# Moving the constants, residuals and tokens of a two-block network to other SBUF addresses

## The reference

```python
mod = silu(c) @ w_mod + b_mod                      # six vectors of 1024: shifts, scales, gates
h, hc = modulate(x, ...), modulate(ctx, ...)       # rmsnorm(t) * (1 + scale) + shift
qkv, z, ba, sc_p, fn_u = split(h @ w_in)           # the same for hc
o_lat = bidir_gated_delta(...)                     # chunked gated delta rule, both directions
merged = g0 * y_dn + g1 * y_sc + g2 * y_fn         # delta, short-convolution and Fourier branches
x = x + gate1 * (merged @ w_o)
x = x + gate2 * swiglu(modulate(x, ...))           # width 2816
x = rmsnorm(x, final_g)
```

## Time and profile before

| | |
|---|---|
| three runs | 2008.36, 2011.93, 2009.1 us; median 2009.1 |
| profiled execution | 2004.89 us, span 2003.1 us |
| instructions | 34324, of these 14672 matmuls |
| TensorE busy | 1833.5 us, 92% of the span |
| VectorE, ScalarE, GpSimd busy | 968.2, 773.9, 463.2 us |
| mean granted TensorE clock | 0.959 |
| moved by DMA | 261.76 MB, 131 GB/s in the mean |

### The profile page before, as it was taken

One profiled execution on the slowest core, in us unless ns is written; L12 is line 12 of the kernel. 1 busy time (PEld: TensorE's weight loads), 2 busy tenths in 40 slices (PEclk: granted clock), 3 DMA queues, 4 the chain that ended last, 5 costly groups with the idle time before them and its releaser, 6 DMA issues.

```text
span 2003.1 us, 34324 instructions
## 1 busy us (share of the span) xinstructions
PE 1833.5 (92%) x14672; PEld 1557.8 (78%) x14672; DVE 968.2 (48%) x1666; ACT 773.9 (39%) x1332; POOL 463.2 (23%) x226
## 2 busy tenths in 40 slices
PE   5998998888899999999798879999999989689999
PEld 3777897877689997877686457787888776479998
DVE  1648425565543335345767754222231247954343
ACT  3453523333345555223532234222222343655443
POOL 0235212122034432211310011121222211013443
PEclk7999998999889998999899989999999999999999
DMA  8343343222465544221210114323322337025553
GB/s 320 156 162 136 105 154 131 86 107 86 170 238 195 190 169 166 101 94 67 85 64 1 64 64 147 126 97 119 122 105 100 111 137 271 3 71 203 190 189 127
DMA packets 36581, 261.76 MB, mean 131 GB/s; under 512 B 4048, under 2 KB 4176, under 8 KB 6224
## 3 DMA queue, kind: packets, MB, share of 16 engines
q1 hardware_dynamic: 36432, 259.58, 35.9%
HBM read 258.51 MB, written 1.05 MB: 130 GB/s over the span
## 4 chain that ended last, share of the span: by engine, by line
PE 77%; DVE 13%; ACT 4%; issue 3%; DMA 1%; POOL 1%; SPq 0%; DVEq 0%; ACTq 0%
PE ps L808 18%; PE ps L810 18%; PE ps L809 18%; PE ps L835 2%; PE ps L859 2%; PE ps L1308 1%; PE ps L1311 1%; DVE msq L2365 1%; PE ps L1077 1%; PE ps L825 1%; PE ps L1065 1%; PE ps L826 1%; PE ps L827 1%; PE ps L922 1%; PE ps L867 1%
## 5 line engine op out<-in xcount | busy, mean ns | idle before, releaser
L726 POOL TENSOR_TENSOR wl<-raw,wh 128x1024 fp32r<-128x1024 f32 (+1 forms) x179 | 428.2, 2395 | 1335.1 <-ACT wh L1417 1335.1
L808 PE MATMUL ps<-h_hi,wh 128*128 128x256 f32 (+1 forms) x1696 | 554.6, 327 | 5.2 <-POOL wl L726 3.8
L810 PE MATMUL ps<-h_hi,wl 128*128 128x256 f32 (+1 forms) x1696 | 544.8, 321 | 0.0
L809 PE MATMUL ps<-h_lo,wh 128*128 128x256 f32 (+1 forms) x1696 | 543.9, 321 | 0.0
L1417 ACT ACTIVATE wh<-raw 128x1024 fp32r<-128x1024 f32 (+1 forms) x330 | 342.4, 1041 | 392.3 <-PE ps L810 283.8
L808 PEld LDWEIGHTS ps<-h_hi,wh 128*128 128x128 f32 x1696 | 322.8, 190 | 35.2 <-POOL wl L726 8.4
L809 PEld LDWEIGHTS ps<-h_lo,wh 128*128 128x128 f32 x1696 | 322.5, 190 | 27.4 <-issue 2.7
L810 PEld LDWEIGHTS ps<-h_hi,wl 128*128 128x128 f32 x1696 | 321.9, 190 | 26.2
L1910 DVE TENSOR_TENSOR wl<-raw,wh 128x1024 fp32r<-128x1024 f32 (+1 forms) x151 | 187.9, 1244 | 240.2 <-ACT wh L1417 225.1
L808 PE MATMUL ps<-gh,wh 128*128 128x256 f32 (+1 forms) x528 | 168.2, 319 | 0.0
L810 PE MATMUL ps<-gh,wl 128*128 128x256 f32 (+1 forms) x528 | 166.9, 316 | 0.0
(11 more groups left out here) (404 smaller groups left out, 2808.8 us busy)
## 6 DMA issues: line engine op xcount, KB each, us to landing
raw<-in_mod SPq DMA_DIRECT2D x72, 1024.0 KB, 5.0
raw<-in_ffn_in SPq DMA_DIRECT2D x66, 1024.0 KB, 4.8
raw<-in_ffn_out SPq DMA_DIRECT2D x24, 1024.0 KB, 4.8
raw<-in_w_in SPq DMA_DIRECT2D x16, 1024.0 KB, 4.9
raw<-in_w_gate SPq DMA_DIRECT2D x12, 1024.0 KB, 4.9
raw<-in_w_ab SPq DMA_DIRECT2D x12, 1024.0 KB, 4.8
raw<-in_ffn_out SPq DMA_DIRECT2D x12, 768.0 KB, 4.4
raw<-in_w_at SPq DMA_DIRECT2D x5, 1024.0 KB, 4.9
```

The costliest lines, as they stand in the source:

```text
L726: nc.gpsimd.tensor_tensor(wl[e % SPLIT][:, 0:entries[e]["words"]], part(e), wh[e % SPLIT][:, 0:entries[e]["words"]].bitcast(F32), ALU.subt ...
L808: nc.tensor.matmul(b[:, cols], wh[e % SPLIT][:, w], xh(k), start=(k == 0), stop=False)
L809: nc.tensor.matmul(b[:, cols], wh[e % SPLIT][:, w], xl(k), start=False, stop=False)
L810: ins = nc.tensor.matmul(b[:, cols], wl[e % SPLIT][:, w], xh(k), start=False, stop=(k == nk - 1))
```

## The change

Two lines are added in the allocation. Each raises the count of words to the next multiple. No instruction is added, removed or moved, and no other offset is changed; tiles placed by `at` follow `phase_at`, `h_at`, `arena` and `spare`.

```diff
     small = sb("small", [P, NSMALL + (-NSMALL) % 8])
+    words[0] += -words[0] % 64
     call = sb("const_all", [P, NCALL])
     phase_at = words[0]
     c1 = sb("const_1", [P, NC1])
...
     words[0] += T - L - P - 8
+    words[0] += -words[0] % 256
     res_c = sb("res_c", [P, KD, L])
     res_l = sb("res_l", [P, KD, L])
     h_at = words[0]
```

## The result

The changed kernel takes 2022.55 us in the median of 7 runs (2017.45 to 2028.94), the kernel before 2011.16 in 7 runs beside it: the ratio is 1.0059, with a 95% interval of 1.0042 to 1.0076. It is slower, by some 12 us; the forecast was no change that can be told.

What follows compares the result with a forecast made beforehand. The prediction took TensorE's rate through 14672 matmuls to bound the kernel (busy 92%), plus stretches where VectorE finishes last. Its terms summed 0 + 0 + 0 + 0, so it forecast the unchanged median, 2009.1 us, range 2003.5 to 2015.

Steps and rivals of the forecast that it cites:

- the one under TensorE: 7536 matmuls streaming moved tiles: same step at either address, 117.8 against 117.7 ns; taken as 0, bound 1.1 us either way.
- The sign of being wrong that the prediction named: Dense stretches' matmul count in 10 us moved by one or more everywhere, or a moved-tile operation with another median.
- is not fixed by the address: TensorE's surplus over plain column time: 91 or 87 matmuls in 10 us with the same tokens at the same addresses.
- Rival 1: Tokens and weights at the same position modulo 256 words slow 7536 matmuls by 2 ns each, 15.1 us, giving 2024; 5%.
- Rival 2: Operands starting mid 128-byte piece cost one piece more; matmuls lose the surplus, 42 + 53 us, giving 1914; 2%.
- The other terms: Everything beside TensorE: VectorE and ScalarE 0 (bound 0.5 us), GpSimd 0 (bound 2.1), DMA 0 (bound 2).
- VectorE, ScalarE and GpSimd 0: Operations on moved tiles keep their times: 0, bounds 0.5 us for VectorE and ScalarE, 2.1 us for GpSimd's 40 level products.
- the constants 0: Constants move from word 12688 to 12736; their loads fall under the transfers taken as 0, with no separate time priced.
- the reading of the edit as one shift by 48 words: Everything from the constants up moves 48 words (192 bytes); the second new line adds nothing.
- DMA: Loads and stores of moved tiles, 7.5 of 260 MB: 0, bounds 0.1 us by pieces of a row, 2 us by whole transfer.

Runs made afterwards that it cites:

- all_up_48: Every tile, weight buffers too, moved up 48 words against the kernel before, so the token-to-weight distance stays 208; ratio 1.0003 (0.9977 to 1.0029).
- weights_208_rest_256: Against the kernel before, weight buffers and `small` moved up 208 words, all else 256, making the distance 0; ratio 1.0075 (1.0052 to 1.0097).
- before_again: The kernel before, unedited, run again as a control; ratio to the kernel before 1.0006 (0.9985 to 1.0027).
- const_only_48: Against the kernel before, constants and small tiles behind them up 48 words; residuals, tokens and arena up 256, keeping distance 208; ratio 0.9986 (0.9967 to 1.0005).
- after_again: The changed kernel, unedited, run again as a control; ratio to the kernel before 1.0068 (1.0042 to 1.0093).
- res_only_48: Against the kernel before, only residuals, tokens and arena moved up 48 words, constants left in place, distance 0; ratio 1.0069 (1.0051 to 1.0088).
- by_stretch: Against the kernel before, distances chosen by stretch: middle layer 0, first block, attention layer and outer feed-forwards 16 (modulo 64 words); ratio 1.0005 (0.9988 to 1.0022).
- h_hi_0_h_lo_16: Against the kernel before, `h_hi` and the arena set at distance 0 modulo 64 words to the weights, `h_lo` alone at 16; ratio 1.0076 (1.0039 to 1.0112).
- dist_240: Against the kernel before, residuals, tokens and arena up 32 words, distance 240 (48 modulo 64); ratio 1.0049 (1.0027 to 1.0071).

## Why the prediction was wrong

**The step that failed** is the one under TensorE: "no difference", 0 with a bound of 1.1 us either way. It compared the by-token stretch, where `wh` and `wl` stream and the tokens are loaded, with the feed-forward, where `gh` and `gl` stream and `wh` and `wl` are loaded. I took that as today's position against tomorrow's. It is so for one operand, but what counts is the distance of the two. That was -208 words in the one and 208 in the other, 48 and 16 modulo 64, and 0, which the change brings, was in neither. `all_up_48` and `weights_208_rest_256` show that the quantity compared is the one without effect.

That the two agreed within 0.15 ns was luck besides. At 16 and at 48 a stretch has 117.7 or 113.3, and I had read one by-token stretch that had 117.7. Another of the same kind in the same trace had 113.5, over 94 steps:

```profile
834.05 0.28 PE L826 MATMUL ps<-wl,h_hi 128*128 128x256 f32 x1
...
844.72 0.28 PE L827 MATMUL ps<-wh,h_lo 128*128 128x256 f32 x1
```

The 0.15 ns were the resolution of one reading and not the spread between stretches, and the bound of 1.1 us made from them was no bound. The sign of being wrong that the prediction named did come: in 30 us, 268 and 257 matmuls became 252 and 253.

**What the runs put in its place.** Four profiles are at 16 (before, before_again, all_up_48, const_only_48) and four at 0 (after, after_again, weights_208_rest_256, res_only_48); these are means of each four, counted as in the table. The 4800 dense matmuls of 256 columns went from 117.4 to 120.0 ns, +12.3 us; the 480 by-token ones from 115.3 to 119.9, +2.2 us; the 2736 of 512 columns from 228.9 to 226.9, -5.6 us. That is 8.9 us. The spans of the same profiles have means 2010.5 and 2021.9, 11.4 us apart, and differ by up to 14 us inside each four.

The rest has the size of a second difference, in the clock. Span x (1 - mean granted clock) went from 85.0 to 88.5 us in these profiles. Over all runs the mean granted clock was 0.9553 in 41 runs of the five kernels at 0 and 0.9584 in 123 runs at 16, with standard errors of 0.0004 and 0.0003. By the same estimate that is 6.8 us, of the 13.3 by which the mean times differ. With the 8.9 us of the steps it makes a little more than the whole, as it may, since TensorE doesn't set the pace everywhere. The 38 runs at the other distances have 0.9579; the two mixed layouts, with part of their 512-column stretches at 226.7, have 0.9563 (`by_stretch`) and 0.9566 (`h_hi_0_h_lo_16`). That the faster 512-column stretches bring the clock down is a guess that no run here isolates.

**The two profiles alone** would have told it with the wrong weights. They differ by 12.7 us; 7.3 of these lie in the first feed-forward, where the profile before had the rarer 113.3 and the one after has 120.0. Its 1103 steps from behind the first two tiles to the norm put between took 125.1 us there, 130.0 in the second profile of the same kernel, and 132.4 after the change. The prediction noticed 91 against 87 matmuls in 10 us and took from it that the surplus "is not fixed by the address". The surplus has both: the layout gives the possible values, and which of them a stretch gets differs between stretches and executions.

**Rival 1** had the mechanism in part, the relation of the two operands, at 5% and 15.1 us. It failed in the sign for 512 columns, and it priced the matmul by 2 ns from a load and dismissed it because L1042's matmuls kept 275 ns. Those have 128 columns, a length whose dependence on the distance no run here isolated. It should have had far more than 5%: no row of the trace showed a dense stretch at distance 0, and what a trace can't show must be bounded from something else, not set to 0.15 ns. Rival 2 also fails: the surplus over 213.3 fell by 2.2 ns and not by 15.5.

**The other terms** held as far as a run can tell: VectorE, ScalarE and GpSimd 0, as the rows above show, the constants 0 (const_only_48), the reading of the edit as one shift by 48 words (res_only_48 gives the same steps by itself). For DMA nothing is shown: the loads above differ by 0.8 us and more at one position.

**TensorE's two reads.** The Trainium skill, page "SBUF — State Buffer", section "SBUF: two separate sides", says that among the engines only the port pair shared by VectorE and GpSimd causes contention and that TensorE never waits on anyone; its table gives the moving operand and the weight load independent reads. Here TensorE's step with unchanged instructions goes from 117.7 to 120.0 ns, or from 229.0 to 233.4, by the distance of the two operands alone. That the two reads meet in some part of the memory is my reading; no run shows what they meet in.

## What to carry to other kernels

- When only addresses change, ask first which operands are read at the same time and what the change does to their distance, not where one of them lies. A comparison inside one trace says nothing about a value of that quantity that none of its stretches has.
- Read the rate of dense matmuls from starts over long stretches, in several profiles: 2 ns in 118 are invisible in a busy share and 0.6% of the kernel, and one execution can have another value for the same code. Read the granted clock of all runs beside it: what the steps gained in `by_stretch` didn't show in the time.
- Rounding tile addresses to large powers of two is no default for speed: here it made all distances 0, and a distance of 16 words was the better one for this mix of shapes.

## What the runs showed of the hardware that was not expected

- The step of a dense fp32r matmul with a weight load beside it depends on the distance of the moving operand from the loaded one, with its sign, for the nine distances tried (modulo 64 words, by the one pair 0 and 64): 256 columns 115.9 to 120.0 ns, 512 columns 226.9 to 234.3 in the mean.
- The best distance depends on the length: 0 and 24 are the worst for 256 columns (120.0), and 0 is the best for 512 (226.9).
- At 16 and 48, a 256-column stretch runs at 117.7 or 113.3 ns, and the same stretch can change between executions. At 16 the share of dense triples at 113.3 was 27% in the first profile and 5, 3 and 1% in the others. At 48 it was 57, 73, 57 and 39% of the by-token ones in the same four profiles, and 43% of the dense ones in dist_240. At 0 such stretches ran at 120.0 in all five profiles.
- Two operands of one triple at different distances are slower than both at either: 232 ns against 226.7 and 229.0.
- The runs of one kernel spread by more than the effect: 1998.9 to 2022.4 us for the kernel before. The mean granted clock in the changed kernel's runs goes along with it, 0.959 in the run of 2017.45 us and 0.951 in that of 2028.47.
- Kernels at distance 0 had a lower mean granted clock than those at 16, 0.9553 against 0.9584, with the same instructions. Why is open.
